# The output projection of a hybrid decoder layer: three fp32r products of split operands, the 64-row tile first, and the routing and expert buffers reordered behind it

## The reference, cut to what matters

```python
merged = (g[:, :, 0] * (z @ lp['w_br_ssm']) + g[:, :, 1] * (o_swa @ lp['w_br_swa'])
          + g[:, :, 2] * (o_mem @ lp['w_br_mem']))
x = x + merged @ lp['w_out']                       # (576, 1024) @ (1024, 1024)
x = x + hier_moe(rmsnorm(x, lp['norm2_g']), lp)
# hier_moe: best group of 4 by softmax of x @ w_rg, then 2 of its 8 experts by softmax of x @ w_rexp
for e in range(N_EXPERTS):                         # 32 experts, 1024 -> 256 -> 1024
    h = jax.nn.silu(xt @ lp['w_e_gate'][e]) * (xt @ lp['w_e_up'][e])
    y = y + combine[:, e:e + 1] * (h @ lp['w_e_down'][e])
y_prompt, y_sample = rmsnorm(xp, final_norm_g), rmsnorm(xs, final_norm_g)
```

## Time and profile before

| | |
|---|---|
| three runs, us | 901.63, 901.88, 904.59; median 901.88 |
| profiled execution, us | 900.25 (span 898.5) |
| mean granted TensorE clock | 0.965 |
| TensorE busy | 788.0 us, 88% of the span |
| VectorE / ScalarE busy | 39% / 22% |
| expert chunks | 96 of 1 MB |

### The profile page before, as it was taken

The page is one execution under the profiler, slowest core; times in us unless marked ns, Lnnn a source line. Parts: engine busy times, 40 slices in busy tenths (PEclk is TensorE's granted clock), DMA queues, the critical chain, the costliest instruction groups (busy, mean ns, idle before and its releaser), DMA issues. The chain is left out here.

```text
span 898.5 us, 11563 instructions
## 1 busy us (share of the span) xinstructions
PE 788.0 (88%) x4443; PEld 572.2 (64%) x4443; DVE 350.9 (39%) x831; ACT 200.8 (22%) x377; POOL 78.7 (9%) x107
## 2 busy tenths in 40 slices
PE   5999999999999899999899999993999977767730
PEld 4887887779788566679899988872333322322210
DVE  2597566661600567348344123445111111101118
ACT  2320300002242244446242002122111110110103
POOL 0100230001011000000000000012011101001000
PEclk9999999999999999999999999995999999999975
DMA  9461283211456332310232259136899999999846
GB/s 363 160 199 48 71 86 109 70 71 61 165 189 235 116 139 96 142 48 1 94 133 103 94 211 419 53 129 256 328 420 420 421 420 422 419 421 421 361 147 235
DMA packets 34117, 186.29 MB, mean 207 GB/s; under 512 B 6000, under 2 KB 6272, under 8 KB 16952
## 3 DMA queue, kind: packets, MB, share of 16 engines
q1 hardware_dynamic: 21712, 146.63, 41.3%
q0 software_dynamic: 11488, 35.45, 12.9%
q10 hardware_dynamic: 864, 3.47, 1.0%
HBM read 176.66 MB, written 17.22 MB: 216 GB/s over the span
## 5 line engine op out<-in xcount | busy, mean ns | idle before, releaser
L455 PE MATMUL ps<-sb 128*128 128x288 f32 (+12 forms) x3214 | 633.2, 425 | 63.1 <-DMA sb<-in_wexp 36.1
L455 PEld LDWEIGHTS ps<-sb 128*128 128x128 f32 (+5 forms) x3214 | 421.2, 168 | 247.3 <-issue 147.4
L455 PE MATMUL ps<-sr 128*128 128x288 f32 x816 | 109.7, 296 | 1.2 <-DVE sr L1706 1.2
L455 PEld LDWEIGHTS ps<-sr 128*128 128x128 f32 x816 | 108.6, 188 | 1.4 <-DVE sr L1706 1.4
L464 PEld LDWEIGHTS ps<-sb 128*128 128x128 f32 (+3 forms) x413 | 43.4, 142 | 41.3 <-issue 35.9
L464 PE MATMUL ps<-sb 128*128 128x128 f32 (+3 forms) x413 | 55.2, 273 | 10.8 <-DMA sb<-xn_rows,sb 7.9
L1922 DVE SCALAR_TENSOR_TENSOR sb<-sb,ps 128x256 f32<-128x256 f32 x16 | 6.7, 421 | 139.1 <-ACT sb L1292 139.1
L1930 DVE COPY sb<-ps 128x1024 f32<-128x1024 f32 x16 | 19.6, 1225 | 70.1 <-PE ps L455 70.1
L1694 DVE SCALAR_TENSOR_TENSOR sb<-sb,ps 128x576 f32<-128x576 f32 x24 | 18.1, 752 | 70.2 <-PE ps L455 70.2
L1015 ACT ACTIVATE sb<-ps 128x576 f32<-128x576 f32 (+4 forms) x29 | 22.9, 790 | 96.5 <-PE ps L455 66.9
L1287 ACT ACTIVATE sb<-ps 128x256 f32<-128x256 f32 x16 | 6.1, 384 | 130.4 <-PE ps L464 130.4
(11 more groups left out here) (240 smaller groups left out, 420.6 us busy)
## 6 DMA issues: line engine op xcount, KB each, us to landing
sb<-in_wexp SPq DMA_DIRECT2D x96, 1024.0 KB, 28.0
sb<-in_wstream SPq DMA_DIRECT2D x34, 1024.0 KB, 4.9
sb<-in_mkT POOLq DMA_DIRECT2D x8, 512.0 KB, 7.3
sb<-in_mv POOLq DMA_DIRECT2D x8, 512.0 KB, 5.2
sb<-expert_rows SPq DMA_DIRECT2D x8, 512.0 KB, 8.3
sb<-in_xT ACTq DMA_DIRECT2D x4, 576.0 KB, 9.1
sb<-in_x SPq DMA_DIRECT2D x4, 512.0 KB, 7.3
sb<-k_pad POOLq DMA_DIRECT2D x8, 256.0 KB, 11.7
```

What stands on the lines that cost most here:

```text
L455: return signed(nc.tensor.matmul(*a, **kw))
```

## The change

- Tile 0 is now the 64-row tile of sample tokens, then the four prompt tiles (`WROWS`, `WTOK`). All code behind the projection takes rows and token offsets from these.
- The 64-row tile is computed first, in plain fp32, side by side, as jobs `w00` and `w20`. The other four tiles are three fp32r products each, 24 matmuls of 256 columns per job.
- ScalarE makes eight high copies of the merged sum (512 columns each, beside `g11a` to `g15b`) and four of the `w_out` blocks. VectorE makes the lows: of the sums behind the merges of `p9` to `p15`, in place; of the `w_out` blocks in place too, so after the fp32 jobs that read them.
- The highs take buffers into which expert chunks 0 to 8 went early. Now chunks 0 to 2 are issued behind `p15`, 3 at `gate_used` 16, 4 to 11 two at a time as blocks of `w_out` are used for the last time (in tile 4), 12 and 13 when the last tile's squares are summed, 14 on as before.
- The order of jobs behind each tile is new: `x2T` of the tile before stands behind `w0`, its logits behind `w1`, its ranks behind `w3`.

```diff
+WROWS, WTOK = [64, 128, 128, 128, 128], [512, 0, 128, 256, 384]
-SLOTS_E = [O_A + 2048 * j for j in (4, 2, 0, 1, 7, 8, 3, 5, 6)] + [O_SM] + [O_W + 2048 * j for j in (2, 3, 0, 1)]
-SLOTS_E += [O_X, O_X + 2048, O_TH]
+SLOTS_E = [O_A + 2048 * j for j in (3, 5, 6)] + [O_SM]
+SLOTS_E += [a for b in range(4) for a in (O_W + 2048 * ((NBLOCKS - 4 + b) % RING), HI_AT["w", b])]
+SLOTS_E += [O_A + 14336, O_A + 16384, O_X, O_X + 2048, O_TH]
+    jobs += ["w00", "w20"]
+    for t in range(1, TT):
+        jobs += [f"w0{t}", f"x2T{t - 1}"] + ([f"tb{t - 2}"] if t >= 2 else [])
+        jobs += [f"w1{t}", f"lg{t - 1}", f"w2{t}", f"w3{t}", f"rk{t - 1}"]
+    jobs += ["x2T4", "tb3", "lg4", "rk4", "tb4", "cnt"]
 # SyncE
-            for n in range(9):
-                if n == 1:
-                    filled(sp, "g15b")
-                if n == 6:
-                    filled(sp, "p15")
+            filled(sp, "p15")
+            for n in range(3):
                 chunk(n, 2 * CHUNKS[n][1] + CHUNKS[n][3])
             sp.wait_ge(gate_used, 16)
-            chunk(9, 2 * CHUNKS[9][1] + CHUNKS[9][3])
-            for n in range(10, 14):
-                sp.wait_ge(w_used, NBLOCKS - 13 + n)
+            chunk(3, 2 * CHUNKS[3][1] + CHUNKS[3][3])
+            for b in range(4):
+                sp.wait_ge(w_used, NBLOCKS - 3 + b)
+                for n in range(4 + 2 * b, 6 + 2 * b):
+                    chunk(n, 2 * CHUNKS[n][1] + CHUNKS[n][3])
+            sp.wait_ge(ss2, TT)
+            for n in range(12, 14):
                 chunk(n, 2 * CHUNKS[n][1] + CHUNKS[n][3])
 # TensorE
+            for b in (0, 2):
+                w_out[b], w_out[b + 1] = weights(), weights()
+                take(f"w{b}0")
+                side_by_side(f"w{b}0", O_Q, [(w_out[b], 256), (w_out[b + 1], 256)]).then_inc(ps_ready, 1)
+            for t in range(1, TT):
                 for b in range(4):
-                    rows_of(f"w{b}{t}", 0, w_out[b], 256, 256, O_Q, t).then_inc(ps_ready, 1)
+                    if t == 1:
+                        pe.wait_ge(lo_ready, LOWS.index(("w", b)) + 1)
+                    for kt in range(KT):
+                        last = three(pat(pair(job), 0, (1, 256)), MH_AT[kt] + WTOK[t], O_Q + kt * T + WTOK[t],
+                                     HI_AT["w", b] + kt * 256, w_out[b] + kt * 256, kt == 0, kt == KT - 1, 256)
+                    if t == TT - 1:
+                        owed.append((w_used, 1))
 # ScalarE
+                    if q in ("g11a", "g12a", "g13a", "g14a", "g15a"):
+                        high_sum(int(q[1:-1]) - 11)
+                    if q == "g14b":
+                        high_weights(("w", 0))
+                    if q == "g15b":
+                        high_weights(("w", 1))
+                        for d in range(5, 8):
+                            high_sum(d)
+                        high_weights(("w", 2))
+                        high_weights(("w", 3))
             for t in range(TT):
-                if t == TT - 1:
+                if t == 0:
                     shift(0)
+                    shift(2)
 # VectorE
+            for b in (0, 2):
+                filled(dve, f"w{b}0")
+                low_weights(("w", b))
+                add_sides(b)
+                low_weights(("w", b + 1))
+            norm(0)
+            for t in range(1, TT):
                 add_h(0, t)
                 if t >= 2:
+                    add_table(t - 2)
                 add_h(1, t)
+                choose(t - 1)
                 add_h(2, t)
                 add_h(3, t)
+                place_rows(t - 1)
```

More of the change, by code:

```diff
@@ L205, in block_index @@
 def block_index(block):
+    if block[0] == "w":
+        return NBLOCKS - 4 + block[1]
     return NBLOCKS - 4 - len(BRANCH_BLOCKS) + BRANCH_BLOCKS.index(block)
@@ L455, in mm, with three @@
                 return signed(nc.tensor.matmul(*a, **kw))
[L457 to L461, removed]
+            def three(out, w_hi, w_lo, x_hi, x_lo, start, stop, n=TH):
+                mm(out, r32(w_hi, 128), r32(x_hi, n), start=start, stop=False)
+                mm(out, r32(w_hi, 128), r32(x_lo, n), start=False, stop=False)
+                return mm(out, r32(w_lo, 128), r32(x_hi, n), start=False, stop=stop)
             def turn_tile(*a):
@@ L763, in piece @@
                 if is_late(name):
-                    pe.wait_ge(lo_ready, SPLITS.index(blk) + 1)
+                    pe.wait_ge(lo_ready, LOWS.index(blk) + 1)
                     wh = HI_AT[blk]
@@ L865, in _ @@
             w_out = [None] * 4
-            for t in range(TT - 1):
-                for b in range(4):
-                    if t == 0:
-                        w_out[b] = weights()
-                    take(f"w{b}{t}")
-                    rows_of(f"w{b}{t}", 0, w_out[b], 256, 256, O_Q, t).then_inc(ps_ready, 1)
-                    if b == 0 and t >= 2:
-                        ranks(t - 2)
-                    if b == 1 and t >= 1:
+            for b in (0, 2):
[3 more added lines that the diff above has]
+            for t in range(1, TT):
+                for b in range(4):
+                    job = f"w{b}{t}"
+                    take(job)
+                    if t == 1:
[3 more added lines that the diff above has]
+                                     HI_AT["w", b] + kt * 256, w_out[b] + kt * 256, kt == 0, kt == KT - 1, 256)
+                    last.then_inc(ps_ready, 1)
+                    if t == TT - 1:
+                        owed.append((w_used, 1))
+                    if b == 0:
                         turn_norm(t - 1)
-                    if b == 1 and t >= 2:
-                        table(t - 2)
-                    if b == 2 and t >= 1:
+                        if t >= 2:
+                            table(t - 2)
+                    if b == 1:
                         logits(t - 1)
-            for b in (0, 2):
-                take(f"w{b}4")
-                side_by_side(f"w{b}4", O_Q, [(w_out[b], 256), (w_out[b + 1], 256)]).then_inc(ps_ready, 1)
-                owed.append((w_used, 2))
-                if b == 0:
-                    ranks(2)
-                    turn_norm(3)
-                    table(2)
-            logits(3)
+                ranks(t - 1)
             turn_norm(4)
+            table(3)
             logits(4)
-            ranks(3)
-            table(3)
             ranks(4)
@@ L1702, in low @@
             def low(what, src, hi, n):
-                k = SPLITS.index(what) + 1
+                k = HIGHS.index(what) + 1
                 dve.wait_ge(hi_ready, k)
@@ L1709, in low_weights, with low_sum @@
                 low(block, O_W + (block_index(block) % RING) * WB, HI_AT[block], WB)
+            def low_sum(d):
+                low(("m", d), O_Q + d * T, MH_AT[d], NP_)
             n_units = len(UNITS)
@@ L1744, in _ @@
                     if q == "p9":
+                        low_sum(0)
                         low_weights(("g", 7))
                     if q == "p10":
+                        low_sum(1)
                         low_weights(("p", 3))
+                    if q == "p11":
+                        low_sum(2)
+                    if q == "p12":
+                        low_sum(3)
+                        low_sum(4)
+                    if q in ("p13", "p14", "p15"):
+                        low_sum(int(q[1:]) - 8)
             c.settle()
@@ L1762, in add_sides @@
             def add_sides(b):
-                job = f"w{b}4"
-                h = [at(O_H + 4 * D + (b + i) * 256, (1, 256), pn=64) for i in range(2)]
+                job = f"w{b}0"
+                h = [at(O_H + (b + i) * 256, (1, 256), pn=64) for i in range(2)]
                 if b == 0:
-                    dve.wait_ge(ld_x4, 16)
+                    dve.wait_ge(ld_kv[0], 16 * 5)
                 filled(dve, job)
@@ L1770, in add_sides @@
                 dve.wait_ge(side_ready, b // 2 + 1)
-                c.free(v.scalar_tensor_tensor(h[1], at(M_THE + b * 128, (1, 256), pn=64), 0.5, h[1], ALU.mult, ALU.add), job)
+                c.free(v.scalar_tensor_tensor(h[1], at(R_SIDE + b * 128, (1, 256), pn=64), 0.5, h[1], ALU.mult, ALU.add), job)
                 c.settle()
```

114 lines of the change are left out of this document (55 added, 59 removed).

## The result

| | median, us | runs | ratio to the kernel before, 95% |
|---|---|---|---|
| before | 901.80 | 20 | |
| changed kernel | 903.98 | 20 | 1.0024 [1.0015, 1.0033] |
| changed kernel, repeated | 903.74 | 12 | 1.0026 [1.0014, 1.0039] |

The change costs 2.2 us. That is a loss, though under the 0.3% that the prediction took as the bound of a difference. The forecast was 900.2: the time lies in the range, the sign is wrong. The ratios are taken over undisturbed executions that ran beside each other, so they are not quite the quotients of the medians.

A forecast was written before the change was run, and what follows sets the result against it. The DMA-paced last stage, started by the first gather's landing, was taken to bound the kernel: -0.5 there and -1.2 at the end sum to -1.7 us, giving a 900.2 us median; range 895.3 to 905.2, likeliest no measurable change.

The forecast's parts named there:

- What sets the end: Last stage: runs at DMA pace, so whatever moves the first gather's landing moves the end by the same amount.
- The pace of 0.120: Projection on TensorE: each 256-column fp32r matmul takes 0.120 us, 46.1 us for 384, 9.9 less than before.
- Rival 3: Projection: loading the stationary tile sets the pace, 0.134 us a matmul; total +3.7 us, median 905.6; chance 0.12.
- The stall at `w20`: Projection's start: TensorE stands 4.8 us until block 33 lands at 536.6.
- `w20` in 3.65 us: Second side-by-side job, behind the stall: priced at 3.65 us, 32 records of 0.114 us.
- rival 2: Slower: the clock falls in the stall before `w20`, which takes 7.3 us; total +0.9 to +3.1 us; chance 0.15.
- VectorE's stall of 1.75: Ahead of tile 0's transposes: TensorE stands another 1.75 us for VectorE's lows and `add_sides(2)`.
- The tail to the write: Routing behind the projection: last job ends at 600.5, write of `xn_rows` is issued at 606.3.
- The write in 8.1: Last 512 KB write of `xn_rows`: lands after 8.1 us behind chunks, at 614.4; the gather waits for it, not the lists.
- Rival 1: Faster: write and gather share the engines with chunks, the lists decide; -5.2 to -6.5 us, median near 896; chance 0.27.
- The gather in 9.3: First gather: issued at 614.6, lands 9.3 us later at 623.9, 0.5 us earlier than before.
- The end, -1.2: First `expert_rows` read: tile 0 is half as large, lands 1.25 us earlier, VectorE's chain starts with it; together -1.2.

The follow-up runs named there:

- sides: Changed kernel plus 24 useless matmuls in the stall before `w20`, `shift(0)` ahead of block 33's copy, `add_sides(2)` ahead of block 32's low: 900.71 us, 0.9993 of before.
- hold: Changed kernel with chunks 10 to 13 issued behind the last write of `xn_rows`, not ahead of it: 900.88 us, 0.9993 of before.
- late14: Changed kernel with chunks 14 to 16 waiting until the first gather has landed: 900.68 us, 0.9991 of before.
- sides_late: Changed kernel with the edits of sides and late14 together: 897.01 us, 0.9953 of before.
- fill_late: Changed kernel with fill, 11 of clock's matmuls ahead of `w01`, `add_sides(2)` ahead of block 32's low, and late14: 897.89 us, 0.9964 of before.
- again: The changed kernel run once more, unchanged: 903.74 us, 1.0026 of before.
- gf: Changed kernel with the 512 KB read of the final gain behind tile 0's two `expert_rows` reads, not ahead: 903.45 us, 1.0028 of before.
- clock: Changed kernel with 24 useless matmuls in TensorE's stall before `w20`: 903.17 us, 1.0015 of before.
- plain: Changed kernel with tiles 1 to 4 in plain fp32, without the splits; order, buffers and chunk issues kept: 914.39 us, 1.0141 of before.
- fill: Changed kernel with job `w01` moved between `w00` and `w20`, and `shift(0)` ahead of block 33's copy: 904.97 us, 1.0032 of before.
- sides_hold: Changed kernel with the edits of sides and hold together: 899.51 us, 0.9975 of before.

## Why the prediction was wrong

Its steps, in their order:

- **What sets the end: right, to within some 2 us.** From the gather's landing to the last scatter's the kernels lie between 243.3 and 246.4 us, while the landing itself moves over 17 us. Measured behind the projection's start, the landings of the five kernels **sides**, **hold**, **late14**, **sides_late** and **fill_late** are 2.3 to 7.0 us earlier than in **again**, and their medians 2.9 to 6.7 lower. One by one the two differ by up to 1.6 us (**hold**: 4.5 and 2.9). The last stage is longest where the gather is earliest (246.1 in **sides_late** and **fill_late**), but the profiled execution of **sides_late** was the slowest of its six, so it stays open whether a part of an early landing is lost again.
- **The pace of 0.120: off by 0.004.** 0.124 from start to start, so a full tile takes 15.1 us, not 14.85. Since no ranks stand behind the last one, the last three come to only +0.35; `w01` is +0.3. Rival 3 (0.134) is out.
- **The stall at `w20`: right in place, 5.5 for 4.8.** +0.7. Block 33 lands 9.1 behind the start (539.8), not 8.5. That is 8.4 us behind its issue at 531.4; the block before it, with no chunks behind it, took 5.1. Whether the first four chunks, issued from 531.9 on, make the difference was not run: no experiment holds them back, though this would shorten the stall instead of filling it.
- **`w20` in 3.65 us: wrong, the mechanism that failed.** The forecast priced the job behind the stall at the full clock. It took 6.20, rival 2's mechanism at the place that it named, +2.5; in **again**, **hold**, **late14** and **gf**, which have the same stall, it took 5.21 to 6.41. Rival 2 had 0.15. What was held against it was a stall of 1.6 us that did nothing, though it put its own point of decision near 5 us, where the forecast stall of 4.8 lay. Its total (+0.9 to +3.1 us) holds what was measured, but by luck: it has the transposes 2.6 to 4.8 us later than forecast, and they came 1.8 later (18.5 behind the start for 16.65), the late block and the pace included; the rest is made up by terms further down. The Trainium skill (TensorE: Matmul & The Clock Gate, Part 1) takes the slow clock for the default, which only activity lifts. The windows agree: 0.55 at the stall's end, 0.50 behind it, 1.00 again from 546.
- **VectorE's stall of 1.75: absent, covered by the slow `w20`.** -1.75; **clock** shows it at 1.40 once `w20` is fast, and there the clock falls behind it instead. So the wrong price of `w20` is worth net +0.8 here, and filling the stall alone would not have got it back. With 0.2 gained in tile 1 the terms so far give +1.9, as measured (74.28 for 72.35).
- **The tail to the write: 6.3 us for 5.8.** +0.5.
- **The write in 8.1, the wait of POOL for it: right.** 8.3, and **hold** (3.9) shows that the chunks make it. Rival 1 fails here: write and chunks did not share as it had it. POOL then needs another 0.9 us to issue where 0.2 was counted. Together +0.9.
- **The gather in 9.3: right**, 8.4 to 9.1; **late14** (5.6) shows that the three chunks make it. -0.9 to -0.2. From the projection's start to the landing 95.8 us were forecast and 98.2 to 98.4 measured.
- **The end, -1.2: wrong, the largest single term by net size.** It gave -0.2 and +0.2. Halving a read of two 512 KB transfers left it at 6.33 us (6.84 in the repeat) for 6.28. Why those bytes bring nothing there stays open; in **gf**, where tile 0 does come earlier, the next tile decides.
- **Not forecast:** the first pair's first 32 records stay at half clock for longer, 9.69 us (again 9.43) for 8.66, which is more than the +0.8 and +0.4 of the last stage. Over the other kernels of the table the same group took 8.5 to 10.1 us where its row stands whole, so the change need not be its cause.

So 0.5 gained before the gather turned into 1.9 to 2.1 lost, and 1.2 at the end into nothing. Forecast -1.7, measured +2.2: in the two profiles the terms come to 4.2 and 4.4 (2.4 and 2.6 before the gather, 1.0 and 1.4 at the end, 0.8 and 0.4 in the last stage), and in the medians to 3.9. No one step carries it: before the gather +0.7 is the late block, +0.8 the clock less the stall that it covers, +0.65 the pace, +1.4 the tail, the write and POOL's issue, against the gather's -0.9 to -0.2 and 0.2 in tile 1. The steps that failed are the full clock behind the stall and the 1.2 us at the end; the others are sizes.

## What to carry to other kernels

A stall on TensorE costs more than its length where the clock falls in it: count the job behind it at half pace (here 5.2 to 6.4 us for 3.7), and when a stall is filled, look at which engine is next in line, because the slow job was that engine's cover. A faster stage pays only if the transfers that hang on its end are not queued behind prefetches; here one wait ahead of three prefetch transfers, first used by later pairs, was worth 3.1 us, more than the change lost. And a smaller or earlier read at the end is to be counted as a gain only if the next read is not what the end waits for then, as it was in **gf**.

## What the runs showed of the hardware

- The granted clock fell in or behind waits of 4.8 to 6.0 us (changed kernel, **hold**, **plain**), but also of 2.54 and 3.11 (**fill**) and 1.40 (**clock**), and did not behind 0.99 and 1.47 (**fill_late**) or the 1.64 ahead of `w00`. Behind one of 0.86 us it fell within the last logits in **sides_hold** (3.22 us) and held in the changed kernel (1.98). The length of one wait does not tell it.
- A write of 512 KB on POOL's queue lands after 3.6 to 3.9 us with at most the end of an earlier chunk on its way and after 7.9 to 8.3 behind chunks; the first gather after 4.7 to 5.6 with no chunk issued beside it and 8.2 to 9.1 with three to seven (7.2 before, where the three went out 3 to 4 us ahead of it). Nearly twice the time for the same bytes, in both.
- An fp32r matmul of 256 columns takes 0.124 us and one of 288 columns 0.134, so columns still count at 256; a record of 40 fp32 columns takes 0.119.
